# Softmax of a head group drawn into the tile behind its scores, with transposes and value products one tile earlier, in a hybrid attention block

## What is computed

```python
proj = rms_norm(x, norm_mix) @ w_in
qa, ka, va, qf, kf, vf, f_logit = split(proj)
qa, ka = rope(qa), rope(ka)
# group A: 16 heads, 4 key heads, window of 2 chunks of 64 tokens, a sink logit per head
s = where(valid, qa @ ka.T / 8, -1e30);  m = max(max(s), sink)
w = exp(s - m) / (sum(exp(s - m)) + exp(sink - m));  out_a = w @ va
# group B ("fox"): 16 heads, causal, with a bias from cumulated log-forget gates
s = where(causal, qf @ kf.T / 8 + F[t] - F[s], -1e30);  out_b = softmax(s) @ vf
x = x + concat(out_a, out_b) @ w_o
```

## The kernel before

| step | DVE | ACT | PE, behind the tile |
|---|---|---|---|
| 14 | maxima of A (L722 to L726) | | |
| 15 | bias and maxima of fox p = 0 (L736, L741) | exponentials of A (L494, L496) | |
| 16 | the same for p = 1 | exponentials of p = 0 (L503) | |
| 17 | normalize A (L746 to L750) | exponentials of p = 1 | |
| 18 | normalize p = 0 (L755, L759) | copy of A turned (L508) | transposes of A (L1091) |
| 19 | normalize p = 1 | copy of p = 0 (L512) | transposes of p = 0 (L1099) |
| 20 | | copy of p = 1 | transposes of p = 1 |
| 21 | | | value products (L1071, L1082) |
| 22 | `mix_lo` (L766) | `mix_hi` (L516) | |

## Time and profile before

### The profile page before, as it was taken

How to read it: one execution, slowest core, us unless ns; L and a number is a source line. 1 busy time by engine, 2 the same in 40 slices (tenths; PEclk the granted TensorE clock), 3 DMA queues, 4 the chain that set the end, 5 groups by cost and what they waited for, 6 DMA issues and landing times.

```text
span 1092.9 us, 18564 instructions
## 1 busy us (share of the span) xinstructions
PE 1078.6 (99%) x6553; PEld 949.1 (87%) x6553; DVE 710.0 (65%) x1023; ACT 579.8 (53%) x889; POOL 26.3 (2%) x42
## 2 busy tenths in 40 slices
PE   9999999999999999999999999999999999999997
PEld 8999999998888888888888888888888888888885
DVE  4666565656555777777877777777777445454543
ACT  6847474636445655555555655555555434343432
POOL 1150000000000000000000000000000000000000
PEclk9999999999999999999999999999999999999999
DMA  8684555554455566665666566656666665555552
GB/s 265 187 270 143 172 144 164 152 164 144 164 183 174 173 188 196 195 189 173 203 191 183 171 209 192 192 173 194 192 198 210 206 191 191 187 188 188 193 189 100
DMA packets 169796, 201.69 MB, mean 185 GB/s; under 512 B 8580, under 2 KB 136292, under 8 KB 169632
## 3 DMA queue, kind: packets, MB, share of 16 engines
q1 hardware_dynamic: 168464, 197.49, 58.0%
q0 software_dynamic: 976, 3.37, 0.9%
q10 hardware_dynamic: 320, 0.34, 0.1%
HBM read 199.06 MB, written 2.11 MB: 184 GB/s over the span
## 4 chain that ended last, share of the span: by engine, by line
PE 94%; ACT 2%; DVE 1%; DMA 1%; issue 0%; SPq 0%; DVEq 0%; ACTq 0%
PE tr_ps L1211 15%; PE acc L1211 15%; PE acc L1213 8%; PE tr_ps L1213 8%; PE acc L963 7%; PE acc L965 7%; PE acc L964 7%; PE sc_ps L963 5%; PE sc_ps L965 5%; PE sc_ps L964 5%; PE tr_ps L963 4%; PE tr_ps L965 4%; PE tr_ps L964 4%; ACT prob L494 1%; DMA nat<-x 1%; ACT hi L419 1%
## 5 line engine op out<-in xcount | busy, mean ns | idle before, releaser
L645 DVE TENSOR_TENSOR lo<-raw,hi 128x1024 fp32r<-128x1024 f32 (+1 forms) x368 | 449.2, 1232 | 291.4 <-ACT hi L419 291.0
L419 ACT ACTIVATE hi<-raw 128x1024 fp32r<-128x1024 f32 (+1 forms) x368 | 384.6, 1058 | 276.4 <-PE acc L965 92.1
L1211 PE MATMUL tr_ps<-act_split,hi 128*128 128x512 f32 x704 | 245.3, 391 | 0.0
L1211 PE MATMUL acc<-act_split,hi 128*128 128x512 f32 x704 | 245.0, 391 | 0.0
L1213 PE MATMUL acc<-act_split,lo 128*128 128x256 f32 x704 | 197.1, 280 | 0.0
L1213 PE MATMUL tr_ps<-act_split,lo 128*128 128x256 f32 x704 | 197.1, 280 | 0.0
L1211 PEld LDWEIGHTS acc<-act_split,hi 128*128 128x128 f32 x704 | 131.7, 187 | 28.9
L1211 PEld LDWEIGHTS tr_ps<-act_split,hi 128*128 128x128 f32 x704 | 131.7, 187 | 28.8
L1213 PEld LDWEIGHTS tr_ps<-act_split,lo 128*128 128x128 f32 x704 | 133.1, 189 | 0.1
L1213 PEld LDWEIGHTS acc<-act_split,lo 128*128 128x128 f32 x704 | 133.1, 189 | 0.0
L963 PE MATMUL acc<-act_split,hi 128*128 128x256 f32 x416 | 119.0, 286 | 0.0
(11 more groups left out here) (206 smaller groups left out, 1294.0 us busy)
## 6 DMA issues: line engine op xcount, KB each, us to landing
raw<-w_up SPq DMA_DIRECT2D x176, 512.0 KB, 4.3
raw<-w_down SPq DMA_DIRECT2D x88, 512.0 KB, 4.3
raw<-w_in SPq DMA_DIRECT2D x72, 512.0 KB, 3.7
raw<-w_o SPq DMA_DIRECT2D x32, 512.0 KB, 3.7
nat<-x SPq DMA_DIRECT2D x8, 256.0 KB, 6.6
key_bias<-nft_dram POOLq DMA_DIRECT2D x4, 512.0 KB, 9.0
result<-nat SPq DMA_DIRECT2D x7, 256.0 KB, 3.0
gfin<-norm_final POOLq DMA_DIRECT2D x1, 1024.0 KB, 8.9
```

The lines of the kernel that those rows point to most:

```text
L419: act.activation(hi[:, slot, 0:n], raw[:, slot, 0:n], ACT.Copy).then_inc(hi_done, 1)
L645: dve.tensor_tensor(lo[:, slot, 0:n], raw[:, slot, 0:n], hi[:, slot, 0:n].bitcast(F32), ALU.subtract).then_inc(lo_done, 1)
L1211: pe.matmul(up_banks[v][b].rearrange("p (a n) -> p a n", a=2), wh[:, c, b * P:(b + 1) * P], act_split[:, :, k, :], start=k == 0, stop=Fals ...
```

## The change

The constants that say in which step each part of the attention is done are changed: all of DVE's statistics (A, fox p = 0, fox p = 1) and A's exponentials go to step 14, normalizing A to 15, fox's exponentials to 15 and 16, its normalizing to 16 and 17, the transposes to 17, 18 and 19, the value products to 20 and their evacuation to 21. ACT gets one more instruction in step 3 of quad 0, an exponential of one column whose result nobody reads.

```diff
-DVE_MAX_A = 14
-DVE_READ = {15: 0, NEXT: 1}
-ACT_EXP_A = 15
+SOFTMAX = 14
...
-PE_VALUES = NEXT + 5
+PE_VALUES = NEXT + 4
...
+                    elif s == 3:
+                        act.activation(small[:, 24:25], eps, ACT.Exp)
                     attention(s, j)
...
-                if s in DVE_READ:
-                    p = DVE_READ[s]
+                for p in range(2) if s == SOFTMAX else ():
                     dve.wait_ge(fq_s, q + 1)
                     dve.wait_ge(bias_s, 4)
                     dve.wait_ge(sf_s, q * 2 + (p + 1))
```

More of the change, by code:

```diff
@@ L65 @@
 PE_SCORES = 13
-DVE_MAX_A = 14
-DVE_READ = {15: 0, NEXT: 1}
-ACT_EXP_A = 15
[L69 to L73, removed]
-PE_VALUES = NEXT + 5
-EVACUATE = NEXT + 6
+SOFTMAX = 14
+DVE_NORM_A = 15
+ACT_EXP = {15: 0, NEXT: 1}
+DVE_NORM = {NEXT: 0, NEXT + 1: 1}
+TURN_A = NEXT + 1
+TURN = {NEXT + 2: 0, NEXT + 3: 1}
+PE_VALUES = NEXT + 4
+EVACUATE = NEXT + 5
 X_THEN = [3, 7, 11]
@@ L489, in attention @@
             def attention(s, q):
-                if s == ACT_EXP_A:
+                if s == SOFTMAX:
                     act.wait_ge(maxa_s, q + 1)
@@ L716, in attention @@
             def attention(s, q):
-                if s == DVE_MAX_A:
+                if s == SOFTMAX:
                     dve.wait_ge(quad_s, q + 1)
```

## The result

The changed kernel takes **1088.89 us** (median of 5, 1088.71 to 1089.29) against 1094.18 (median of 5, 1094.01 to 1096.59): 5.29 us less. The ratio, taken of the means of the two sets of times, is 0.9947 with a 95% interval of 0.9933 to 0.9962, which is 4.2 to 7.3 us; the medians alone give 0.9952. Forecast were 1089.2 and a range of 1088.5 to 1091.6. The profiled execution took 1088.71 us.

What follows compares the result with a forecast made beforehand. PE, busy 1078.6 of 1092.9 us, was taken as the bound, so only its waits count. Removing 4.97 us of them with nothing added gave 1089.85 for the profiled execution, 1089.2 as median; range 1088.5 to 1091.6.

Steps and rivals of the forecast that it cites:

- The sum of 4.97 us: PE's waits at A's transposes (2.22, 0.72, 0.72 us) and at the output projection's start (1.31) all go.
- the bound only: Upper bound of the gain: matmuls restarting faster without waits, 0.1 us more at each of four sites, 5.4 off.
- quad 0's wait: PE's wait at the first transposes of A, 1.5 us longer than the others, put down to a 1.28 us table load.
- The chain: DVE and ACT's new order in quad 1: A normalized at 147.9, PE asks at 150.21, slack 2.3 us.
- 1.2 us of forecast slack: Output projection: ACT finishes A's exponentials at 251.2, PE asks at 252.38; the smallest slack of all.
- The split of tile 18: Sign on DVE in the changed profile: this split about 2.2 us later against tile 14 than now.
- the load of the table: Sign on ACT: table load at about 50.5 to 51.8 us, ahead of a split still starting near 52.4.
- the last one of the sum: Whole kernel: 1094.82 less 4.97 is 1089.85 for the profiled execution, 0.64 above the median, so 1089.2 us.
- The rule on DVE's drains: Skill's rule of a drain after each DVE operation; by it step 14's statistics have large gaps, time about 1100 us.
- The first: Rival at the output projection: it still waits for ACT, only 3.66 us off, 1090.5 us; chance 5%.
- the second: Rival at A's copy or fox's transposes: a new PE wait brings 2.4 us back, 1091.6 us; chance 8%.
- The third: Rival at A's transposes: DVE's unbroken run is slower, A 2.7 us late, four times, 1100.0 us; chance 3%.

Runs made afterwards that it cites:

- the load alone: The kernel before with only the added exponential in step 3 of quad 0: 1092.97 us against 1095.58, ratio 0.9983.
- the kernel with four reductions: The changed kernel with four unread DVE reductions of 1024 elements added at the end of step 14 in each group: 1101.24 us, ratio 1.0053 to the kernel before.
- more products at the start: The changed kernel with unread warming products raised from 8 to 10 and, behind the second transposes, 6 to 10: 1088.94 us; with the first raise only, 1089.95.

## What the prediction had right, and the step that failed

**The bound and the waits.** Behind the start of the program PE's waits were the whole matter, and each went 1:1 with the time. The sum of 4.97 us was measured as 5.09 on the path; the 0.11 that it lacks is the slower first matmul behind the output projection's wait, which I had put into the bound only. The forecast of 1089.2 lies 0.3 us above the median of 1088.89. Of the 1.5 us by which quad 0's wait was the longer, the prediction gave all to the table load; the load alone was worth 1.29.

**The chain.** Laid along quad 1's clock, A was to be ready 2.3 us before PE asks; the trace has 2.35 for that group, the kernel with four reductions 2.24, and 2.1 to 2.5 over all groups. A's exponentials at the output projection had 1.2 us of forecast slack: they end at 246.29 + 0.24 = 246.53 and PE starts at 247.72, 1.2 us. The split of tile 18 comes 2.2 us later, the load of the table at 49.5 and not 50.5 only because the whole start was a microsecond earlier.

**The step that failed is the last one of the sum**, "4.97 us off, nothing added": it takes all of the time outside the waits as fixed, between the profiled execution and the runs and between the two kernels, and the range ends at 5.4 us off. It is not fixed. The start of the program varied over the thirteen profiles by 2.5 us (the scores of quad 0 start between 79.73 and 82.25), up to 1.6 with the start of the row at 10 us and 1.6 with PE's clock. The kernel before had one slow execution in five, 1096.59, which was not profiled; the changed kernel had none. That one execution adds 0.47 us to the mean of the kernel before; without it the means differ by 5.3 us. With it they differ by 5.8, which is 1088.4, 0.1 below my range. How many slow starts fall among five executions is chance. The three times of the kernel before (1094.15 to 1096.59) already showed this spread, and the lower end of the range used it nowhere. The profile of before happened to have a start 1.0 us longer than that of after; only 5.1 of the 6.1 us between the spans are the change's.

**The rule on DVE's drains.** The trace of the changed kernel shows DVE's run without gaps of that kind: from the split at 134.25 to the end of the normalizing at 144.65 it is 10.4 us, as added up from starts in the trace. The Trainium skill's rule (VectorE: DVE Perf Modes, The DRAIN you can't avoid) would, as an estimate, have made it several microseconds longer. The prediction cited it by half: the same section goes on that a next operation which is not held starts earlier. The rows, where the split at 134.25 lasts 1.23 us and the maxima start 1.15 us behind its start, fit that sentence and not the first.

**The rivals.** The first (the output projection keeps its wait) and the second (a new wait at the copy of A) did not happen. The third was right in its price up to the slack: at 4.5 us of padding the kernel is slower than before. It priced the waits alone, as four times the lateness; the four waits came to 9.1 us for a chain 2.1 to 2.4 us late, and the clock took 1.5 more in each of two groups, which it left out. What the prediction gave to moving the transposes, a slack that shrinks, is what it cost; it could have asked whether the move was needed, and it was not. In its account of the added exponential it was right that the load is hidden in step 3, but it did not see that with A's exponentials in step 14 the load would have been hidden where it stood.

**What stays open.** Whether the kernel before's slowest executions (5 of 37 in the three sessions above 1096.3 us, up to 1098.84) are those in which its 2.0 us wait in quad 0 let the clock fall was not shown: its one profile has the full clock there. Whether more products at the start keep the slow starts away is open too: five executions without one are few, and the changed kernel had five such as well.

## What to carry to other kernels

When one engine is bound and the others run ahead of it by a fixed number of tiles, what counts is when the chain between its own instructions is finished: put the chain ahead of work that has slack to spare (here splits three tiles ahead) and check the slack of both. Ask for the result later rather than earlier; in this kernel moving the consumer up with the producer won nothing, and with a late producer the loss went round through every engine that stood in order behind it. And before a gain of half a percent is judged, subtract the part of the span ahead of the first changed instruction.

## What the runs showed that I had not expected

- A wait of about 2 us of PE, in the midst of dense work, was followed by 3 to 4 us at a granted clock of half in two of four places (after 1.93 and 2.06 us), and not in the others (2.07 and 2.24 us), nor behind the 2.00 us in the profile of the kernel before. Where it came it cost another 1.5 us on top of the wait. At the start of the program it followed waits of 2.29 and 2.45 us and not one of 2.20.
- At the start of the program PE's transposes run at half rate in some executions (four in 1.09 us) and at the full one in others (0.63), with the same 16 matmuls ahead of them.
- A table load between the split and A's exponentials moved the chain by its 1.28 us and no more (1.29 measured across the transposes). The Trainium skill, page ScalarE: Activation LUTs, section What ACT_TABLE_LOAD costs, adds a drain of about 1.38 us to each; the measurement disagrees with it here.
- Moving the transposes one tile (2.88 us) too early cost 27 us over four groups, 12.0 of it the direct waits, 10.9 across fox's transposes, 3.6 between them where the clock was low.
- A table load ahead of an activation that must wait for another engine ran in that wait and cost nothing: ACT's wait was 2.83 us without it and 1.53 with it.
